# Seven-product feed-forward on one core: in the first unit the third and fourth product change places, and VectorE makes the fourth's input difference first

## The chip, the core and the metric

The kernel runs on one NeuronCore of one Trainium2 chip. The metric is the device time of one execution in microseconds (us), from runs on the chip; less is better. The core's engines run apart and meet at semaphores: TensorE (PE in the profile, with its weight loads as PEld), VectorE (DVE), ScalarE (ACT), GpSimd (POOL) and SyncE (SP), which issues most of the DMAs.

## The reference

A first network of two layers works on 256 tokens of width 1024: a feed-forward, a mixer (two attentions and a gated delta rule), a second feed-forward. A second network of two layers follows, with a context stream beside it, and its own feed-forward. All is float32. What bears on this change are the feed-forwards:

```
def swiglu(h, w_gu, w_down):
    gate, up = jnp.split(h @ w_gu, 2, axis=-1)
    return (jax.nn.silu(gate) * up) @ w_down

def squared_relu_mlp(h, w1, w2):
    return jnp.square(jax.nn.relu(h @ w1)) @ w2

for l in range(DEPTH):                                   # first network
    x = x + 0.5 * swiglu(rmsnorm(x, ffn1_norm[l]), ffn1_w_gu[l], ffn1_w_down[l])
    x = x + hybrid_mixer(rmsnorm(x, mix_norm[l]), ...)
    x = x + 0.5 * swiglu(rmsnorm(x, ffn2_norm[l]), ffn2_w_gu[l], ffn2_w_down[l])
ctx = ctx + cgt2 * squared_relu_mlp(modulate(rms_norm(ctx, g2), csh2, csc2), w1, w2)
x = x + gt2 * squared_relu_mlp(modulate(rms_norm(x, g2), sh2, sc2), w1, w2)
```

The squared-ReLU form runs once for the context and twice for x, so there are seven feed-forwards in all.

## The kernel before

Each feed-forward is cut into units (17 in the first network, 16 in the second), one slot of weights each. A unit is a matrix product done in the seven-product way of Strassen and Winograd: the weights are four quarters `a11, a12, a21, a22`, the input is `low` (its first four tiles) and `high`, each split into tokens 0 to 127 (`tok0`) and 128 to 255 (`tok1`). Three differences of the input serve all the up units: `t1 = low[tok1] - low[tok0]`, `t2 = high[tok1] - t1`, `t4 = high[tok0] - t2`; a fourth, `high[tok1] - low[tok1]`, is written over `low[tok1]`. VectorE makes them, four instructions of 128x512 in each feed-forward, and counts each on `x_diffs`. It also makes four sums of weight quarters in each unit, counted on `sums_made`: two in `early_sums` (the second, L2077, puts `a11 - a21` over `a21`), one in `sum_two` (L2091), one in `sum_four` (L2097).

TensorE runs the products of unit k in the order p1 and p2 (`raw`), p6, p7, p5 (`middle`), then p1 and p2 of unit k+1, then p4 and p3 (`end`). So the third product is p6, the fourth p7. p6 takes t2 and the sum of L2091; p7 takes `low[tok1]`'s difference and the sum of L2077, and writes another PSUM bank (`v_bank`, in `spots`) than p1, p6, p5 and p3, which add up in one (in `units`). Between p6 and p5 ScalarE copies that bank out (`u2_kept`): p5 may not start before. After p5 it is copied again (`u4_kept`).

```
e_.wait_ge(*p6_done.at(c, base + k + 1))
activate(u2s[k % 2], mu_bank(c, which, k), ACT.Copy).then_inc(u2_kept.handle, 1)
```

All engines run this order as written; there is no scheduler. In the first network TensorE also sums up squares for the norm (`square_sums`, L813) in the first unit: before p6 in the very first one, right behind p6 in the other three. ScalarE waits for that sum, makes Ln and Exp of it (`res_root`), and only then comes to the copy `u2_kept`. In the very first unit it waits, ahead of the copy, for the condition vector from DRAM (`cond_here`). The four first-network units hold eight matrix instructions of 128x256 in a product in the trace; the three of the second network sixteen of 128x128.

Of the kernel before, what the change touches and what calls it, by code (L numbers as in the profile page):

```python
# [21 lines left out]
ALU = mybir.AluOpType  # L22
# [4 lines left out]
P = 128  # L27
T = 256
# [262 lines left out]
def build(nc, stream, x_in, ctx_in, cond, positions, vec1, vec2, bada, consts, tables, out):  # L291
    with ExitStack() as ctx:
# [6 lines left out]
        def signal(name, first=0, **counts):  # L299
            return Signal(sem(name), counts, first)  # L300
# [109 lines left out]
        w_bank, v_bank = spot[:, 4, 0:T], spot[:, 5, 0:T]  # L410
# [11 lines left out]
        p1_done, p2_done, p4_done, p5_done, p6_done, p7_done = (signal(f"product{i}_done", **MUS) for i in (1, 2, 4, 5, 6, 7))  # L422
        p3_done = signal("product3_done", SLOTS, **MUS)
        sums_made = signal("weight_sums_made", **{k: 4 * n for k, n in MUS.items()})
        c1_kept, u2_kept, u4_kept = (signal(f"{n}_kept", **MUS) for n in ("c1", "u2", "u4"))
        c11_made, c21_made = (signal(f"{n}_made", 1, **MUS) for n in ("c11", "c21"))
        c22_made = signal("c22_made", **MUS)
        x_taken = signal("chain_bank_taken", 2, **MUS)
        x_diffs = signal("input_differences_made", one=8, ctx=4, two=4)
# [107 lines left out]
        def input_sum(c, which):  # L537

            if which:
                return c, 1  # L540
            return (Place("one", c.turn - 1), 2) if c.turn else (Place("load"), 0)
# [8 lines left out]
        def mu_half(c, k):  # L550

            return 4 if (c.sec != "one" or k < FFN_UP) else DOWN_HALF[(k - FFN_UP) % 3]
# [4 lines left out]
        def mu_quarters(c, which, k):  # L557


            w, n = slot[(MU_GROUP[c.sec][which] + k) % SLOTS], mu_half(c, k)  # L560
            if k < mu_up(c):
                w = w[:, :].rearrange("p (e k h m c) -> p h m e k c", e=2, k=n, h=2, m=2)
                return w[:, 0, :, 0], w[:, 0, :, 1], w[:, 1, :, 0], w[:, 1, :, 1]
            w = w[:, 0:8 * n * P].rearrange("p (h m k e c) -> p h m e k c", h=2, m=2, k=n, e=2)
            return w[:, 0, :, 0], w[:, 0, :, 1], w[:, 1, :, 0], w[:, 1, :, 1]

        def by_tokens(c, k):

            return c.sec == "one" and k < FFN_UP

        def mu_sum(c, k):

            n = mu_half(c, k)
            return w_sum["one" if c.sec == "one" else "two"][k % 2][:, 0:2 * n * P].rearrange("p (m k c) -> p m k c", m=2, k=n)

        def mu_moving(c, which, k):

            if k < mu_up(c):
                return lambda kt: (act[:, kt, :], act[:, 4 + kt, :], kt)
            chunk = (k - mu_up(c)) % (3 if c.sec == "one" else 4)  # L580
            return lambda kt: (hT[:, 8 * chunk + 2 * kt, :], hT[:, 8 * chunk + 2 * kt + 1, :], 4 * chunk + kt)

        def mu_bank(c, which, k):

            return lin[:, (k + 1 + which) % 2 if c.sec == "one" else k % 2, 0:T]

        def mu_diffs(c, k):

            return x_diff if k < mu_up(c) else h_diff["one" if c.sec == "one" else "two"]
# [167 lines left out]
        def _(pe):  # L757
# [82 lines left out]
            def multiply(c, which):  # L840

                count, up = MUS[c.sec] // len(MU_GROUP[c.sec]), mu_up(c)
                base = count * which
# [7 lines left out]
                def quarter(dst, weights, n, moving, first, rows_=False):  # L851

                    if rows_:
                        for kt in range(n):
                            mm = pe.matmul(dst.rearrange("p (m c) -> p m c", m=2), moving(kt), weights[:, :, kt, :], start=(first and kt == 0),  # L855
                                           stop=(kt == n - 1), skip_group_check=True)
                        return mm
                    for m in range(2):
                        for kt in range(n):
                            mm = pe.matmul(dst[:, m * P:m * P + P], weights[:, m, kt, :], moving(kt),  # L860
                                           start=(first and m == 0 and kt == 0), stop=(kt == n - 1), skip_group_check=True)
                    return mm
# [7 lines left out]
                def raw(k):  # L870
# [22 lines left out]
                    if opening:  # L893
                        square_sums(*input_sum(c, which))

                def middle(k):
                    (a11, _, a21, _), n = mu_quarters(c, which, k), mu_half(c, k)
                    moving, (t1, t2, _) = mu_moving(c, which, k), mu_diffs(c, k)
                    if k == 0:
                        pe.wait_ge(*x_diffs.at(c, 4 * which + 2))  # L900
                    pe.wait_ge(*c1_kept.at(c, base + k + 1))
                    pe.wait_ge(*sums_made.at(c, 4 * (base + k) + 3))
                    quarter(mu_bank(c, which, k), a11, n, lambda kt: t2[:, moving(kt)[2], :], False, by_tokens(c, k)
                            ).then_inc(p6_done.handle, 1)
                    if k == 0 and c.sec == "one" and (c.turn or which):
                        square_sums(*input_sum(c, which))
                    if k == 0:
                        pe.wait_ge(*x_diffs.at(c, 4 * which + 4))
                    pe.wait_ge(*c21_made.at(c, base + k))
                    quarter(v_bank, a21, n, lambda kt: moving(kt)[0][:, P:T], True, by_tokens(c, k)).then_inc(p7_done.handle, 1)  # L910
                    pe.wait_ge(*u2_kept.at(c, base + k + 1))
                    quarter(mu_bank(c, which, k), mu_sum(c, k), n, lambda kt: t1[:, moving(kt)[2], :], False,
                            by_tokens(c, k)).then_inc(p5_done.handle, 1)

                def end(k):
                    (_, a12, _, a22), n = mu_quarters(c, which, k), mu_half(c, k)
                    moving, (_, _, t4) = mu_moving(c, which, k), mu_diffs(c, k)
                    pe.wait_ge(*c22_made.at(c, base + k + 1))
                    quarter(v_bank, a22, n, lambda kt: t4[:, moving(kt)[2], :], False, by_tokens(c, k)
                            ).then_inc(p4_done.handle, 1)  # L920
                    pe.wait_ge(*u4_kept.at(c, base + k + 1))
                    pe.wait_ge(*sums_made.at(c, 4 * (base + k) + 4))
                    quarter(mu_bank(c, which, k), a12, n, lambda kt: moving(kt)[1][:, P:T], False, by_tokens(c, k)
                            ).then_inc(p3_done.handle, 1)
# [559 lines left out]
            def two(c, order):  # L1484
                for step, i in order:
                    if step == "sum":
                        square_sums(c, i)
                    elif step == "lin":
                        plain_two(c, *i)
                    elif step in ("scores", "turn", "values", "out", "early"):  # L1490
                        {"scores": scores_two, "turn": turn_two, "values": values_two, "out": out_two,
                         "early": early}[step](c, i)
                    elif step == "csum":
                        pe.wait_ge(*c21_made.at(Place("ctx"), TWO_MU))
                        square_sums(Place("ctx"), 1)
                    elif step == "klin":
                        key_product(c, i)
                    elif step not in ("norm", "squares", "soft", "gsum", "gmul", "knormed", "ksquare"):
                        rest_two(c, step)
                multiply(c, 0)  # L1500
# [4 lines left out]
            for l in range(DEPTH):  # L1505
                c = Place("one", l)
                multiply(c, 0)
                if l == 0:
                    pe.wait_ge(consts_made, 1)
                mixer(c)  # L1510
                multiply(c, 1)
# [460 lines left out]
        def _(ve):  # L1972
# [106 lines left out]
            def multiply(c, which):  # L2079
                count, up = MUS[c.sec] // len(MU_GROUP[c.sec]), mu_up(c)  # L2080
                base = count * which
# [5 lines left out]
                def sum_two(k):  # L2087
                    a11 = mu_quarters(c, which, k)[0]
                    ve.drain()
                    ve.wait_ge(*p1_done.at(c, base + k + 1))  # L2090
                    ve.tensor_tensor(a11, mu_sum(c, k), a11, ALU.subtract).then_inc(sums_made.handle, 1)  # L2091
# [17 lines left out]
                low, high, tok0, tok1 = act[:, 0:4, :], act[:, 4:8, :], slice(0, P), slice(P, T)  # L2109

                def second_difference():
                    ve.tensor_tensor(t2, high[:, :, tok1], t1, ALU.subtract).then_inc(x_diffs.handle, 1)

                ve.drain()
# [21 lines left out]
                    ve.wait_ge(*normed.at(c, 2 * KD))  # L2136
                    second_difference()
                sum_two(0)
                ve.tensor_tensor(low[:, :, tok1], high[:, :, tok1], low[:, :, tok1], ALU.subtract).then_inc(x_diffs.handle, 1)
                if first and which == 0:  # L2140
                    before, i = input_sum(c, which)
                    if added_up(before, i):
# [561 lines left out]
            for l in range(DEPTH):  # L2704
                c = Place("one", l)
# [171 lines left out]
```

## Time and profile before

| | us |
|---|---|
| median of 3 runs | 2614.05 (2613.34 to 2615.8) |
| the profiled execution, its own time | 2619.14 |
| its span, first to last instruction | 2617.3 |
| PE busy | 2580.3 (99%) |
| PEld busy | 2273.3 (87%) |
| DVE busy | 1390.8 (53%) |
| ACT busy | 746.5 (29%) |
| POOL busy | 19.3 (1%) |

The mean granted TensorE clock is 0.997 of full speed. A row of the timeline gives its start, its length, engine, line, operation, what it writes and reads with shapes, how many instructions are merged, and in brackets how long the engine was idle before and what released it. The seven first units are called A to G here, by the start of p6:

| first unit | part of the network | p6 starts, us |
|---|---|---|
| A | layer 1, first feed-forward | 17.99 |
| B | layer 1, second feed-forward | 622.18 |
| C | layer 2, first feed-forward | 840.80 |
| D | layer 2, second feed-forward | 1443.51 |
| E | context | 1765.70 |
| F | second network, layer 1 | 2092.15 |
| G | second network, layer 2 | 2415.96 |

### The profile page before, as it was taken

Reading aid. Unit: us, or ns where it says so; the run is one execution under the profiler, and the core shown is the slowest. Engines: PE = TensorE matmul, PEld = TensorE weight load, DVE = VectorE, ACT = ScalarE, POOL = GpSimd, SP = SyncE. Lnnn points to the kernel's source line nnn. Section 1 sums busy time; section 2 is a strip of 40 time slices with the busy share of each in tenths; the row PEclk is TensorE's granted clock in tenths of the full one; section 3 lists DMA queues with packets and bytes.
Section 4 is the critical chain, followed back from the end, with each engine's and each line's share of the span. In section 5 each row is a group of like instructions: output and inputs, shape, how many; then the busy total and the mean of one; then the engine's idle time right before and its main releaser. Section 6 shows DMA issues by size and latency. Waiting matters only on the chain.

```text
span 2617.3 us, 46846 instructions
## 1 busy us (share of the span) xinstructions
PE 2580.3 (99%) x19506; PEld 2273.3 (87%) x19506; DVE 1390.8 (53%) x2373; ACT 746.5 (29%) x1825; POOL 19.3 (1%) x33
## 2 busy tenths in 40 slices
PE   9999999999999999999999999999999999999999
PEld 7899778888899889787888889869997799967999
DVE  6674253315666666244422666256663566635665
ACT  4531132112541551123210453231123411133110
POOL 0000000000000000000000000000000000000000
PEclk9999999999999999999999999999999999999999
DMA  7664321145555565431135565424443144431443
GB/s 264 226 226 180 118 89 73 69 158 203 215 218 218 200 231 208 150 121 49 67 121 188 228 225 210 167 97 142 180 170 136 68 150 177 162 129 65 161 162 113
DMA packets 54483, 414.71 MB, mean 158 GB/s; under 512 B 4128, under 2 KB 8480, under 8 KB 34432
## 3 DMA queue, kind: packets, MB, share of 16 engines
q1 hardware_dynamic: 50224, 357.96, 37.2%
q10 hardware_dynamic: 3456, 50.33, 5.2%
q8 instruction: 155, 2.54, 0.4%
q0 software_dynamic: 592, 3.41, 0.4%
q14 instruction: 56, 0.46, 0.0%
HBM read 410.64 MB, written 1.05 MB: 157 GB/s over the span
## 4 chain that ended last, share of the span: by engine, by line
PE 95%; DVE 2%; ACT 1%; DVEq 1%; issue 0%; DMA 0%; ACTq 0%; SPq 0%
PE units L860 19%; PE spots L860 14%; PE units L781 14%; PE units L855 12%; PE spots L855 8%; PE units L986 7%; PE spots L1176 2%; PE units L1287 2%; PE spots L836 2%; PE units L1334 2%; PE units L1452 1%; PE units L964 1%; PE units L957 1%; PE spots L1383 1%; PE spots L1364 1%; PE spots L1373 1%
## 5 line engine op out<-in xcount | busy, mean ns | idle before, releaser
L781 PE MATMUL units<-normed,weights 128*128 128x256 f32 x1040 | 230.6, 382 | 2.2 <-ACT normed L1523 2.2
L1523 ACT ACTIVATE mla_q_rope<-units 128x256 f32<-128x256 f32 (+1 forms) x248 | 95.4, 387 | 461.5 <-PE units L860 368.9
L781 PEld LDWEIGHTS units<-normed,weights 128*128 128x128 f32 x1040 | 197.8, 191 | 32.5 <-issue 5.9
L1523 ACT ACTIVATE hidden<-delta_qkv 32x128 f32<-32x128 f32 x704 | 215.5, 306 | 7.7
L986 PE MATMUL units<-normed,weights 128*128 128x256 f32 x832 | 191.9, 384 | 0.0
L860 PE MATMUL units<-hidden,weights 128*128 128x128 f32 x1472 | 180.9, 276 | 0.0
L860 PE MATMUL spots<-hidden,weights 128*128 128x128 f32 x1472 | 180.1, 275 | 0.0
L986 PEld LDWEIGHTS units<-normed,weights 128*128 128x128 f32 x832 | 154.5, 190 | 28.8 <-issue 8.0
L860 PEld LDWEIGHTS units<-hidden,weights 128*128 128x128 f32 x1472 | 172.1, 192 | 1.6 <-issue 1.6
L860 PEld LDWEIGHTS spots<-hidden,weights 128*128 128x128 f32 x1472 | 172.1, 192 | 0.0
L855 PE MATMUL units<-weights,normed 128*128 128x256 f32 x704 | 167.6, 381 | 1.6 <-DMA weights<-stream 1.6
L855 PE MATMUL spots<-weights,normed 128*128 128x256 f32 x704 | 167.3, 381 | 0.7 <-DMA weights<-stream 0.5
L855 PEld LDWEIGHTS spots<-weights,normed 128*128 128x128 f32 x704 | 134.5, 191 | 20.0 <-DMA weights<-stream 0.9
L855 PEld LDWEIGHTS units<-weights,normed 128*128 128x128 f32 x704 | 132.6, 190 | 21.6 <-issue 4.1
L2097 DVE TENSOR_TENSOR weights<-weights 128x1024 f32<-128x1024 f32 (+1 forms) x116 | 140.0, 1207 | 10.7
L2198 DVE TENSOR_TENSOR delta_new_values<-spots,mla_q_rope 128x256 f32<-128x256 f32 x116 | 49.1, 423 | 176.0 <-PE spots L860 154.2
L2077 DVE TENSOR_TENSOR weights<-weights 128x1024 f32<-128x1024 f32 (+1 forms) x116 | 139.1, 1199 | 0.0
L1523 ACT ACTIVATE delta_state<-units 128x256 f32<-128x256 f32 x116 | 44.6, 384 | 279.2 <-PE units L860 220.2
L781 PE MATMUL units<-hidden,weights 128*128 128x256 f32 x528 | 119.4, 382 | 0.6 <-DVE residual L2689 0.4
L781 PEld LDWEIGHTS units<-hidden,weights 128*128 128x128 f32 x528 | 98.7, 190 | 16.4 <-issue 3.0
L860 PE MATMUL units<-normed,weights 128*128 128x128 f32 x768 | 95.9, 279 | 5.0 <-ACT normed L1523 4.4
L2091 DVE TENSOR_TENSOR weights<-latents,weights 128x1024 f32<-128x1024 f32 (+1 forms) x56 | 67.6, 1207 | 60.0 <-PE units L860 35.0
(389 smaller groups left out, 4160.7 us busy)
## 6 DMA issues: line engine op xcount, KB each, us to landing
weights<-stream SPq DMA_DIRECT2D x138, 2048.0 KB, 7.7
values_mla_qk_mla_values<-stream ACTq DMA_DIRECT2D x24, 2048.0 KB, 8.2
weights<-stream SPq DMA_DIRECT2D x46, 1024.0 KB, 5.2
weights<-stream SPq DMA_DIRECT2D x16, 768.0 KB, 7.1
weights<-stream SPq DMA_DIRECT2D x4, 512.0 KB, 8.7
constants<-consts SPq DMA_DIRECT2D x1, 1094.5 KB, 14.0
residual<-x_in SPq DMA_DIRECT2D x2, 512.0 KB, 5.8
weights<-stream SPq DMA_DIRECT2D x4, 256.0 KB, 5.1
```

The source lines that it names most:

```text
L781: mm = pe.matmul(dst, w[:, kt * width + col:kt * width + col + P], rhs[:, kt, :], start=(kt == 0), stop=(kt == k - 1))
L836: mm = pe.matmul(banks[32 * q:32 * q + 32, 0, 0:P], cond_s[:, kt, :], w, start=(kt == 0), stop=(kt == KD - 1))
L855: mm = pe.matmul(dst.rearrange("p (m c) -> p m c", m=2), moving(kt), weights[:, :, kt, :], start=(first and kt == 0), stop=(kt == n - 1), ...
L860: mm = pe.matmul(dst[:, m * P:m * P + P], weights[:, m, kt, :], moving(kt), start=(first and m == 0 and kt == 0), stop=(kt == n - 1), skip ...
L986: mm = pe.matmul(dst[:, m * T:m * T + T], w[:, col:col + P], act[:, kt, :], start=(kt == 0), stop=(kt == KD - 1), skip_group_check=True)
L1176: mm = pe.matmul(banks[rows_, t, col:col + CHUNK], lhs[rows_, t, e, p, :], stacked[rows_, :] if rhs is None else rhs[rows_, t, e, p, :], s ...
L1287: mm = pe.matmul(dst[:, m * T:m * T + T], w[:, col:col + P], merged[:, kt, :], start=(kt == 0), stop=(kt == KD - 1))
L1334: mm = pe.matmul(dst, act[:, kt, part * P:part * P + P], w[:, kt * 512:kt * 512 + 512], start=(kt == 0), stop=(kt == KD - 1))
L1523: return nc.scalar.activation(dst, src, func, **kw)
L2077: ve.tensor_tensor(a21, a11, a21, ALU.subtract).then_inc(sums_made.handle, 1)
L2091: ve.tensor_tensor(a11, mu_sum(c, k), a11, ALU.subtract).then_inc(sums_made.handle, 1)
L2097: ve.tensor_tensor(a12, a12, a11, ALU.subtract).then_inc(sums_made.handle, 1)
```

## The change

In the first unit of every feed-forward TensorE runs p7 ahead of p6. VectorE makes the difference for p7 right ahead of t2, where it stood behind `sum_two`. The counts that p7 and p6 wait for on `x_diffs` are fitted to that, and the wait for t4 moves from p7 to p4. The other units are as they were.

```
+                def seventh(k, a21, n, moving):
+                    if k == 0:
+                        pe.wait_ge(*x_diffs.at(c, 4 * which + 2))
+                        pe.wait_ge(*sums_made.at(c, 4 * (base + k) + 2))
+                    pe.wait_ge(*c21_made.at(c, base + k))
+                    quarter(v_bank, a21, n, lambda kt: moving(kt)[0][:, P:T], True, by_tokens(c, k)).then_inc(p7_done.handle, 1)
+
                 def middle(k):
                     (a11, _, a21, _), n = mu_quarters(c, which, k), mu_half(c, k)
                     moving, (t1, t2, _) = mu_moving(c, which, k), mu_diffs(c, k)
                     if k == 0:
-                        pe.wait_ge(*x_diffs.at(c, 4 * which + 2))
+                        seventh(k, a21, n, moving)
+                        pe.wait_ge(*x_diffs.at(c, 4 * which + 3))
...
                     if k == 0 and c.sec == "one" and (c.turn or which):
                         square_sums(*input_sum(c, which))
-                    if k == 0:
-                        pe.wait_ge(*x_diffs.at(c, 4 * which + 4))
-                    pe.wait_ge(*c21_made.at(c, base + k))
-                    quarter(v_bank, a21, n, lambda kt: moving(kt)[0][:, P:T], True, by_tokens(c, k)).then_inc(p7_done.handle, 1)
+                    if k:
+                        seventh(k, a21, n, moving)
...
                     pe.wait_ge(*c22_made.at(c, base + k + 1))
+                    if k == 0:
+                        pe.wait_ge(*x_diffs.at(c, 4 * which + 4))
...
                 def second_difference():
+                    ve.tensor_tensor(low[:, :, tok1], high[:, :, tok1], low[:, :, tok1], ALU.subtract).then_inc(x_diffs.handle, 1)
                     ve.tensor_tensor(t2, high[:, :, tok1], t1, ALU.subtract).then_inc(x_diffs.handle, 1)
...
                 sum_two(0)
-                ve.tensor_tensor(low[:, :, tok1], high[:, :, tok1], low[:, :, tok1], ALU.subtract).then_inc(x_diffs.handle, 1)
```

On TensorE, in unit B (layer 1, second feed-forward), the order before, where `spots<-weights1,normed` is p2 at its first place and p7 at its second, `units<-weights1,squares` is p6 and `units<-rows,squares` is p5:

```order
L1287 MATMUL units<-delta_qkv,weights0 128x256 x32
L855 MATMUL units<-weights1,normed 128x256 x4
L855 MATMUL spots<-weights1,normed 128x256 x4
L855 MATMUL units<-weights1,squares 128x256 x4
L813 MATMUL spots<-square_sums,ones 128x256
L855 MATMUL spots<-weights1,normed 128x256 x4
L855 MATMUL units<-rows,squares 128x256 x4
L855 MATMUL units<-weights2,normed 128x256 x4
```

and now:

```order
L1295 MATMUL units<-delta_qkv,weights0 128x256 x32
L855 MATMUL units<-weights1,normed 128x256 x4
L855 MATMUL spots<-weights1,normed 128x256 x8
L855 MATMUL units<-weights1,squares 128x256 x4
L813 MATMUL spots<-square_sums,ones 128x256
L855 MATMUL units<-rows,squares 128x256 x4
L855 MATMUL units<-weights2,normed 128x256 x4
```

p7 now stands right behind p2 (together the x8), and p5 comes directly behind p6 and the sum of squares; C and D read the same, and in A the sum stands ahead of both.

On VectorE, at the same place, the order before, where L2112 makes t2, L2091 is `sum_two`, L2139 makes the difference over `low[tok1]` and L2146 makes t4:

```order
L2003 TENSOR_TENSOR square_sums<-square_sums,squares 128x256 x2
L2112 TENSOR_TENSOR squares<-normed,squares 128x512
L2091 TENSOR_TENSOR weights<-rows,weights 128x2x4x128
L2139 TENSOR_TENSOR normed<-normed 128x4x128
L2146 TENSOR_TENSOR squares<-normed,squares 128x512
L2097 TENSOR_TENSOR weights<-weights 128x2x4x128
```

and now, each line number 8 higher or, from L2112 to L2121, 9 higher:

```order
L2011 TENSOR_TENSOR square_sums<-square_sums,squares 128x256 x2
L2120 TENSOR_TENSOR normed<-normed 128x4x128
L2121 TENSOR_TENSOR squares<-normed,squares 128x512
L2099 TENSOR_TENSOR weights<-rows,weights 128x2x4x128
L2154 TENSOR_TENSOR squares<-normed,squares 128x512
L2105 TENSOR_TENSOR weights<-weights 128x2x4x128
```

The difference of L2139 moved ahead of t2 and of `sum_two` (now L2099); t4 and `sum_four` have the same work ahead of them as before.

## Rows read from the trace of the kernel before

**Rows 1.** The page's chain that ended last, shares of the span by engine.
```profile
PE 95%; DVE 2%; ACT 1%; DVEq 1%; issue 0%; DMA 0%; ACTq 0%; SPq 0%
```

**Rows 2.** Timeline of B: start us, us, engine, line, operation, count [idle before].
```profile
619.46 1.26 DVE L2112 TENSOR_TENSOR squares<-normed,squares 128x512 f32<-128x512 f32 x1
...
621.96 0.68 DVE L2139 TENSOR_TENSOR normed<-normed 128x512 f32<-128x512 f32 x1
...
622.18 3.65 PE L855 MATMUL units<-weights,squares 128*128 128x256 f32 x8 [2.33 <-DVE weights L2091]
622.56 0.68 DVE L2146 TENSOR_TENSOR squares<-normed,squares 128x512 f32<-128x512 f32 x1
...
626.30 0.38 ACT L1523 ACTIVATE rstd<-spots 128x256 f32<-128x256 f32 x1 [6.46 <-PE spots L813]
...
627.26 0.38 ACT L1523 ACTIVATE mla_q_rope<-units 128x256 f32<-128x256 f32 x1
...
627.83 1.89 PE L855 MATMUL units<-rows,squares 128*128 128x256 f32 x8
```

**Rows 3.** Timeline of C, the same columns.
```profile
837.86 1.13 DVE L2112 TENSOR_TENSOR squares<-normed,squares 128x512 f32<-128x512 f32 x1
838.58 0.99 POOL L722 TENSOR_TENSOR square_sums<-square_sums,squares 128x256 f32<-128x256 f32 x1
...
840.80 1.97 PE L855 MATMUL units<-weights,squares 128*128 128x256 f32 x8 [1.51 <-DVE weights L2091]
...
843.23 0.38 ACT L1523 ACTIVATE rstd<-spots 128x256 f32<-128x256 f32 x1 [4.48 <-PE spots L813]
...
844.02 0.37 ACT L1523 ACTIVATE mla_q_rope<-units 128x256 f32<-128x256 f32 x1
...
844.76 1.89 PE L855 MATMUL units<-rows,squares 128*128 128x256 f32 x8
```

**Rows 4.** Timeline of A.
```profile
14.16 1.22 DVE L2076 TENSOR_TENSOR rows<-weights 128x1024 f32<-128x1024 f32 x1 [0.84 <-DMA weights<-stream]
...
15.31 1.22 DVE L2077 TENSOR_TENSOR weights<-weights 128x1024 f32<-128x1024 f32 x1
...
17.99 3.65 PE L855 MATMUL units<-weights,squares 128*128 128x256 f32 x8 [2.91 <-DVE weights L2091]
...
22.37 0.42 ACT L1523 ACTIVATE context_keys<-context_keys 128x256 f32<-128x256 f32 x1 [5.07 <-DMA context_keys<-cond]
...
22.70 0.37 ACT L1523 ACTIVATE mla_q_rope<-units 128x256 f32<-128x256 f32 x1
...
23.20 1.91 PE L855 MATMUL units<-rows,squares 128*128 128x256 f32 x8
```

**Rows 5.** Timeline of E: p6.
```profile
1765.70 2.02 PE L860 MATMUL units<-squares,weights 128*128 128x128 f32 x16 [0.75 <-DVE weights L2091]
```

**Rows 6.** Timeline of F: p2, p6, the copy of ScalarE, p5.
```profile
2090.11 1.95 PE L860 MATMUL spots<-normed,weights 128*128 128x128 f32 x16
...
2092.15 2.02 PE L860 MATMUL units<-squares,weights 128*128 128x128 f32 x16
...
2094.21 0.38 ACT L1523 ACTIVATE mla_q_rope<-units 128x256 f32<-128x256 f32 x1 [3.52 <-PE units L860]
...
2095.79 1.95 PE L860 MATMUL units<-squares,probabilities 128*128 128x128 f32 x16
```

**Rows 7.** Timeline: p1 of E and of G, each behind an idle time.
```profile
1760.29 2.49 PE L860 MATMUL units<-normed,weights 128*128 128x128 f32 x16 [2.21 <-ACT normed L1523]
...
2410.55 3.66 PE L860 MATMUL units<-normed,weights 128*128 128x128 f32 x16 [2.21 <-ACT normed L1523]
```

**Rows 8.** Stretches right behind idle times: A:B, us, PE busy, granted clock, DMA share, GB/s.
```profile
622.20:625.60 3.40, 3.40 (x8) 0.50 0.29 119
1760.30:1763.70 3.40, 3.28 (x23) 1.00 0.52 217
2410.80:2414.20 3.40, 3.40 (x17) 0.50 0.43 183
```

## The prediction, written before the changed kernel ran

> **What bounds the kernel now.** I read the chain of waits first: 95% of the span lies on TensorE [rows 1], so only what delays or frees a matrix product counts, and an instruction moved on VectorE costs nothing unless a product waits behind it. Then I read the timeline around the seven first units. The reader is to see one pattern in it. In B TensorE had p2 done at 619.85 and stood idle for 2.33 us, until `sum_two` had made the weights of p6 [rows 2]. C has the same wait with 1.51 us, A with 2.91, E with 0.75 [rows 3 to 5]. F has hardly any: p6 starts 2.04 us behind p2, where two products behind it together take 3.64, so 1.82 each; 0.22 are lost [rows 6]. D repeats B row for row, 2.33 us idle too, and G repeats F with a still smaller gap. The third thing to read is the second half of the same rows: p5 never waits for its input in B to G, because p7 stands between p6 and p5 and covers ScalarE's copy. The fourth is the clock. Right behind B's gap the granted clock was 0.50 for 3.4 us, which is 1.2 GHz of 2.4; behind C's gap p6 took 1.97 us instead of B's 3.65, so it ran at 2.4 GHz [rows 2, 3, 8].
>
> All starts below are moved on the profiled execution's time line. Its own time was 2619.14 for a span of 2617.3; the median of the runs shown is 2614.05. I form the difference on the trace and add it to the median.
>
> **What the change moves on VectorE.** One instruction, `low[tok1]`'s difference, 0.68 us long, goes ahead of t2 and `sum_two`. Two such in a row start 0.60 apart (L2139 at 621.96, L2146 at 622.56) [rows 2]. So `sum_two` and with it p6 become ready 0.60 later wherever VectorE was busy up to there (B to G). t4, `sum_four` and what follows keep their time, since the same work lies ahead of them. No DMA and no queue of SyncE or GpSimd is passed. In A the move is free: VectorE idled 0.84 there for a weight piece (L2076) [rows 4]. The wait for t4, moved from p7 to p4, is met several products before and costs nothing.
>
> **What it moves on TensorE.** p7 fills the gap ahead of p6, a product's length that is no longer needed later. Against that p5 loses its cover. From now on p5 starts when ScalarE has copied p6's bank. In the second network that is p6's start to the copy's start, 2.06, the copy 0.38, and about 0.13 to the first product (copy end 23.07, p5 at 23.20 in A), so 2.57 instead of 3.64 [rows 4, 6]. In the first network the sum of squares, Ln and Exp stand ahead of the copy on ScalarE's queue. In C: p6 840.80, Ln 843.23, copy 844.02 to 844.39, plus 0.13, gives 3.72 from p6 to p5, where it is 3.96 now [rows 3]. In B Ln to copy is 0.96 and not 0.79 [rows 2], which gives 2.43 + 0.96 + 0.38 + 0.13 = 3.90.
>
> **B and D.** The first of the three VectorE instructions takes 1.26 us in B, stretched beside an add of GpSimd as in C [rows 2, 3]. Now the moved difference is in its place: 619.46 + 1.26 = 620.72, and p7 starts 0.15 later (the trace's usual distance to VectorE's end) at 620.87, behind a gap of 1.02. It ends about 622.8. p6 is ready at 622.18 + 0.60 = 622.78. No gap as long as 2.33 is left, and C's 1.51 brought no fall of the clock, so p6 runs at 2.4 GHz. p5 starts at 622.78 + 3.90 = 626.68, before at 627.83 [rows 2]: a gain of 1.15. All of it comes from the clock: with the clock up p5 would have started at 622.18 + 3.96 = 626.14 before, and the change would then lose 0.54. D the same: in sum 2.3 gained.
>
> **C.** The gap of 1.51 holds p7 nearly whole; p6 starts at 841.40, p5 at 841.40 + 3.72 = 845.12, before 844.76: 0.4 lost [rows 3].
>
> **E, F, G.** In E TensorE is free at 1764.95; p7 takes 1.82, p5 follows 2.57 behind p6: 1769.34. Before it was 1765.70 + 3.64 = 1769.34: nothing [rows 5, 6]. In F p7 could start at 2090.11 + 1.82 = 2091.93, p6 at 2093.75, p5 at 2096.32, before 2095.79: 0.5 lost [rows 6]. G as F: 0.5 lost.
>
> **A.** p5 starts at 23.20 because ScalarE is held until 22.37 by the condition vector's DMA, and only then copies p6's bank (22.70) [rows 4]. Neither moves, so p5 starts at 23.20 again. But p7 can begin at 15.31 + 1.22 + 0.15 = 16.68, p6 follows, and both are done near 20.3 if the clock holds. So TensorE's gap of 2.91 doesn't go, it moves from ahead of p6 to ahead of p5. Before, the two products at 1.2 GHz were hidden by the DMA; now a fall of the clock hits p5 and what follows, all of which lies on the path. The price of a fall is B's p6 to p5, 5.65, less C's 3.96: 1.7 [rows 2, 3]. A gap of 2.91 at this place had a fall (p6 took 3.65) [rows 4], so I count it: 1.7 lost. The bounds are 0 and 1.7.
>
> Sum: -2.3 + 0.4 + 0 + 0.5 + 0.5 + 1.7 = 0.8 us slower, so 2614.05 + 0.8, about 2614.9. The later waits of TensorE are set by VectorE and ScalarE, which follow TensorE's own products, so a shift passes through to the end.
>
> **Two rules weighed.** The rows show that a gap of 2.21 us ahead of E's p1 left the granted clock at 1.00 and one of the same 2.21 ahead of G's p1 brought 0.50 [rows 7, 8]. By the Trainium skill, TensorE: Matmul & The Clock Gate, section "What's actually happening", the observation of activity runs on by itself and does not start anew with the kernel, so where a gap lands decides. By that rule the falls of B and D need not be in the timed runs at all, and neither need A's; the rows of E and G agree with it. It is the second rival below.
> In C the first of VectorE's instructions took 1.13 us and the next GpSimd add ran from 838.58 to 839.57 [rows 3]. The Trainium skill's page SBUF — State Buffer, section "Who interferes with whom", says that a VectorE instruction with two inputs in SBUF and a GpSimd one that reads there block each other for a whole instruction. By that rule t2 in C would start only at 839.57, and C's loss would be 0.7 and not 0.4.
>
> **Rivals.** First, nothing falls in A: the gap ahead of p5 is cut in two by where it lands, or p7 itself runs slowly behind the 1.60 us that stay idle ahead of it and the DMA hides that again. For it: E's gap passed. Against it: both longest gaps of the trace, A's and B's, had a fall. Time: 2614.9 - 1.7 = 2613.2.
> Second, this one clearly on the slower side: the lost cover decides alone. It does so where B's and D's gaps had no fall in the timed runs; then there is no clock to win back, and each loses 0.54 instead of gaining 1.15. Its place is p5's wait for the copy in six first units, its price 0.54 + 0.54 + 0.4 + 0.5 + 0.5 = 2.5, with A's fall 4.2. It decides from the point where p6's start moves by less than the clock had cost. Time: 2616.5 to 2618.2, the middle 2617.4. For it: the runs shown are 3 to 6 us quicker than the profiled one.
> Third, faster: p7 in the gap ends the falls in B and D, A has none, and ScalarE's chain is quicker than I read it, so that nothing is lost in C, F and G: -1.15 - 1.15, time 2611.8. For it: ScalarE is busy for 29% of the span only. Against it: the copy's place behind p6 is in the code and in every row.
> Fourth, new falls: behind p5's new wait, some 1.4 us in B, C and D (p6's start plus about 2.3 of work against 3.7 to 3.9), the clock falls. Each costs 1.7: 2614.9 + 5.1 = 2620.0. Against it: C's gap of 1.51 had none.
> Fifth, the change does not do what it says, p7 waiting for something else (the copy out of its bank, the weights' sum): the order shows that it waits only for work done long before, so this has next to no chance.
>
> **How the numbers follow.** The forecast has 0.40, the first rival 0.15, the second 0.28, the third 0.07, the fourth 0.08, the fifth 0.02. About 0.2%, 5.2 us, is what a measurement of this kernel can tell from no change. The range, 2612.0 to 2618.6, takes in the forecast and the first two rivals and leaves out the third and the fourth, 0.15 of the chance. Faster by over 5.2 us no case reaches: 0.02 for what I don't see. Slower by over 5.2 takes nearly all of the fourth rival (2620.0): 0.06. Within it, 0.92.
>
> **What would show it.** In the changed profile p7 starts within 0.2 us of the moved difference's end in B and D, p6 0.6 later than before, and p5 is released by ScalarE's copy in B to G, with idle time of TensorE ahead of it. In B and D the granted clock stays at 1.00; in A it falls behind 22 us. In A p5 starts at 23.2. If p5 in B starts before 626 or TensorE is not idle ahead of it in C, my reading of ScalarE's queue is wrong; a total beyond 2620 or below 2611 would mean something outside these seven places.

## The result and the profile after

The changed kernel takes 2618.95 us (median of 20 runs, 2618.12 to 2621.17), the kernel before 2615.48 (20 runs, 2613.31 to 2617.73): ratio 1.0016, 95% interval 1.001 to 1.0022, so 3.5 us slower by the medians and some 4 by the ratio, where 0.8 was forecast. 2618.95 lies 0.35 us above the stated range and 4.05 above the forecast of 2614.9; 1.43 of that is the base, since the forecast was added to 2614.05, the median of three runs, and twenty runs gave 2615.48. The profiled execution of the changed kernel took 2618.94 us, its span is 2617.1, and TensorE still carries 95% of the chain [rows 1].

In B the change did what the rows of before promised. Timeline of the changed kernel, same columns as [rows 2]:

```profile
618.61 1.26 DVE L2120 TENSOR_TENSOR normed<-normed 128x512 f32<-128x512 f32 x1
...
619.92 1.99 PE L855 MATMUL spots<-weights,normed 128*128 128x256 f32 x8 [0.93 <-DVE normed L2120]
...
621.93 1.97 PE L855 MATMUL units<-weights,squares 128*128 128x256 f32 x8
...
624.36 0.38 ACT L1531 ACTIVATE rstd<-spots 128x256 f32<-128x256 f32 x1 [5.38 <-PE spots L813]
...
625.32 0.38 ACT L1531 ACTIVATE mla_q_rope<-units 128x256 f32<-128x256 f32 x1
...
625.76 1.99 PE L855 MATMUL units<-rows,squares 128*128 128x256 f32 x8 [1.44 <-ACT mla_q_rope L1531]
```

p7 starts 0.05 us behind the moved difference, p6 runs at full clock (1.97 us), and p5 has a wait of its own, 1.44 us, for ScalarE's copy. p6 to p5 takes 3.83 (3.90 forecast).

In C, against [rows 3], p6 waits 0.55 and p5 1.24:

```profile
839.61 1.97 PE L855 MATMUL units<-weights,squares 128*128 128x256 f32 x8 [0.55 <-DVE weights L2099]
...
843.25 1.99 PE L855 MATMUL units<-rows,squares 128*128 128x256 f32 x8 [1.24 <-ACT mla_q_rope L1531]
```

VectorE there, ahead of p6, with GpSimd's add (POOL) beside the two differences:

```profile
835.88 1.13 DVE L2120 TENSOR_TENSOR normed<-normed 128x512 f32<-128x512 f32 x1
836.61 0.99 POOL L722 TENSOR_TENSOR square_sums<-square_sums,squares 128x256 f32<-128x256 f32 x1
836.94 1.21 DVE L2121 TENSOR_TENSOR squares<-normed,squares 128x512 f32<-128x512 f32 x1
```

t2 took 1.21 us instead of 0.69: it ended 0.55 behind the add. This agrees with the rule of the Trainium skill, SBUF — State Buffer, section "Who interferes with whom", that the prediction weighed. C's measured loss, 0.56, lies between the prediction's two sums, 0.4 and 0.7. The second counted the add's cost as new, but the same add had cost VectorE time before the change too, in `sum_two`, which took 1.57 us there instead of 1.22:

```profile
839.08 1.57 DVE L2091 TENSOR_TENSOR weights<-rows,weights 128x1024 f32<-128x1024 f32 x1
```

With t2 from 839.57, `sum_two` 0.60 later at its plain 1.22 and 0.15 to p6, the second sum comes to 841.54 for p6 and 845.26 for p5, a loss of 0.5 and not 0.7. From the first difference to p6 that is 3.68 us; it measured 3.73.

In A the gap has moved ahead of p5, against [rows 4], but p5 ran at full clock in this record:

```profile
15.77 1.97 PE L855 MATMUL spots<-weights,normed 128*128 128x256 f32 x8 [1.57 <-issue]
...
22.26 1.99 PE L855 MATMUL units<-rows,squares 128*128 128x256 f32 x8 [2.80 <-ACT mla_q_rope L1531]
```

G costs more than the 0.5 forecast. Before, p1 to p6 were 2410.55 to 2415.96, 5.41 us [rows 7]; now it is 7.52, with p7 in between (p2 and p7 are one row). To compare like with like, take p1 to p5, which holds p7 in both orders: 9.06 before and 9.95 now. p5 before:

```profile
2419.61 1.95 PE L860 MATMUL units<-squares,probabilities 128*128 128x128 f32 x16
```

and G now (the view ends inside p5):

```profile
2409.40 3.47 PE L860 MATMUL units<-normed,weights 128*128 128x128 f32 x16 [2.21 <-ACT normed L1531]
2412.66 4.43 PE L860 MATMUL spots<-normed,weights 128*128 128x128 f32 x32
2416.92 1.95 PE L860 MATMUL units<-squares,weights 128*128 128x128 f32 x16
2419.35 0.82 PE L860 MATMUL units<-squares,probabilities 128*128 128x128 f32 x5 [0.47 <-ACT mla_q_rope L1531]
```

The clock, in the columns of [rows 8], is down behind three gaps, of E's p1, of a place near 2294 us that the change doesn't touch (the first projection of the second network's last layer, L781), and of G's p1:

```profile
1758.80:1762.10 3.30, 3.30 (x17) 0.50 0.24 99
2294.70:2298.00 3.30, 3.30 (x10) 0.50 0.28 119
2410.70:2414.00 3.30, 3.30 (x17) 0.50 0.10 40
```

### The profile page after: what moved, and what is told of

It is laid out like the page before. It is cut to its first block, busy times and chain, and to the rows that moved or that the text cites. A ratio compares the mean times of both kernels' runs of the same rounds, so it can differ in the third digit from the quotient of the medians.

```text
span 2617.1 us, 46853 instructions
## 1 busy us (share of the span) xinstructions
PE 2578.7 (99%) x19506; PEld 2270.9 (87%) x19506; DVE 1390.9 (53%) x2373; ACT 746.7 (29%) x1825; POOL 19.2 (1%) x33
## 3 DMA queue, kind: packets, MB, share of 16 engines
HBM read 410.64 MB, written 1.05 MB: 157 GB/s over the span
## 4 chain that ended last, share of the span: by engine, by line
PE 95%; DVE 2%; ACT 1%; DVEq 1%; DMA 1%; issue 0%; SPq 0%; ACTq 0%
PE units L860 19%; PE spots L860 14%; PE units L781 14%; PE units L855 11%; PE spots L855 8%; PE units L994 7%; PE spots L1184 2%; PE units L1295 2%; PE spots L836 2%; PE units L1342 2%; PE units L1460 1%; PE units L972 1%; PE units L965 1%; PE spots L1391 1%; PE spots L1372 1%; DMA context_keys<-cond 1%
## 5 line engine op out<-in xcount | busy, mean ns | idle before, releaser
L781 PE MATMUL units<-normed,weights 128*128 128x256 f32 x1040 | 230.7, 382 | 2.2 <-ACT normed L1531 2.2
L781 PEld LDWEIGHTS units<-normed,weights 128*128 128x128 f32 x1040 | 197.8, 191 | 32.5 <-issue 5.9
L781 PE MATMUL units<-hidden,weights 128*128 128x256 f32 x528 | 119.4, 382 | 0.6 <-DVE residual L2697 0.4
L781 PEld LDWEIGHTS units<-hidden,weights 128*128 128x128 f32 x528 | 98.7, 190 | 16.4 <-issue 3.0
L2099 DVE TENSOR_TENSOR weights<-latents,weights 128x1024 f32<-128x1024 f32 (+1 forms) x56 | 67.6, 1207 | 59.6 <-PE units L860 35.0
```

What stands on the lines that cost most here:

```text
L781: mm = pe.matmul(dst, w[:, kt * width + col:kt * width + col + P], rhs[:, kt, :], start=(kt == 0), stop=(kt == k - 1))
```

## The experiments

"Before" beside a result is the kernel before on the same chip in the same session. Where an experiment's own records are read, the places keep the names A to G.

**before_again.** No edit.

> The kernel before once more, for a second record of where its clock falls. If the first profile was typical of the timed runs: falls in A, B, D, near 2294 and in G again. If it was not (its time, 2619.14, lies above all timed runs): fewer, with B or D or both at full clock, where p6 to p5 then takes 3.96 us instead of 5.65.

It took 2615.42 us, the median of the runs of before beside it, so by its time this record is the typical one. Granted clock behind D's p6 gap, E's p1, the place near 2294 (2292.77 in this record) and G's p1:

```profile
1443.00:1446.40 3.40, 3.25 (x15) 1.00 0.97 410
1758.90:1762.20 3.30, 3.30 (x17) 0.50 0.32 134
2292.80:2296.20 3.40, 3.40 (x16) 1.00 0.55 236
2407.50:2410.80 3.30, 3.30 (x17) 0.50 0.32 134
```

D and the place near 2294 are at full clock here, where the first record had a fall in both; B and A have one again. In D p6 to p5 is 3.96, so the forecast's "with the clock up" case holds there:

```profile
1443.15 1.97 PE L855 MATMUL units<-weights,squares 128*128 128x256 f32 x8 [2.33 <-DVE weights L2091]
...
1447.11 1.89 PE L855 MATMUL units<-rows,squares 128*128 128x256 f32 x8
```

And E had a fall, yet p1 to p6 took 5.53 us, against 5.41 without one in the first record:

```profile
1758.22 3.64 PE L860 MATMUL units<-normed,weights 128*128 128x128 f32 x16 [2.21 <-ACT normed L1523]
1761.65 2.26 PE L860 MATMUL spots<-normed,weights 128*128 128x128 f32 x16
1763.75 1.95 PE L860 MATMUL units<-squares,weights 128*128 128x128 f32 x16
```

TensorE's wait for `sum_two` (0.75 in E, [rows 5]) had swallowed the slow p1.

**change_again.** No edit of the changed kernel.

> The changed kernel once more, on the chip and beside the runs of before that the other kernels share. Theory 1 (lost cover): p5 waits for ScalarE's copy in B, C, D, F and G, some 2.5 us in all, and the falls of the clock in B and D that the profile of before shows are absent from most timed runs, so nothing is won back: 2.5 us slower plus what falls elsewhere add, 2.5 to 4. Theory 2 (clock): the waits themselves cost little; the changed kernel has one or two falls of the clock more than before (A's gap ahead of p5; E and G), 1.7 us each, so its mean granted clock is lower than that of before by 0.0007 or more in the runs, and its times stand in two groups some 1.8 us apart. My forecast's theory (falls in B and D won back) expects 0 to 1 us.

2619.2 us (11 runs) against 2615.28 (31): ratio 1.0016, 1.0007 to 1.0025. Five runs lie at 2620.0 to 2620.9 with a mean granted clock of 0.997, six at 2618.1 to 2619.2 with 0.998. At 0.998 the kernel before averages 2614.9 (14 runs), at 0.997 2616.0 (13 runs). So at equal clock the change still costs 4.0 and 4.6 us: more falls cannot be the main difference. What a fall costs and the lost cover remain. The record is of the upper group, 1.74 above the first one, and in A its p5 ran at half clock:

```profile
22.48 3.44 PE L855 MATMUL units<-rows,squares 128*128 128x256 f32 x8 [3.19 <-ACT mla_q_rope L1531]
```
```profile
22.90:26.20 3.30, 3.30 (x10) 0.50 0.70 293
```

**vector_only.** VectorE's part alone (shortened):

```
 def middle(k):
-    pe.wait_ge(*x_diffs.at(c, 4 * which + 2))       # ahead of p6
+    pe.wait_ge(*x_diffs.at(c, 4 * which + 3))
 def second_difference():
+    ve.tensor_tensor(low[:, :, tok1], high..., low..., ALU.subtract)...   # no longer behind sum_two
```

> Only VectorE's part of the change: low's difference ahead of t2; TensorE keeps p6 before p7. Theory 1: p6 waits for sum_two, so it starts 0.6 us later in B, C, D and E and some 0.4 later in F and G, 3.2 us slower in all, A unchanged; the whole change must then have won about 0.7 back on TensorE. Theory 2: the longer gap ahead of p6 (2.9 in B and D, 2.1 in C) brings falls of the clock too, 4.5 to 8 us slower.

2621.94 us (9 runs) against 2615.28: ratio 1.0025, 1.0015 to 1.0035. The size is that of theory 2, the clock: C's gap grew from 1.51 to 2.30 and now has a fall (p6 3.34 us long).

```profile
843.13 3.34 PE L855 MATMUL units<-weights,squares 128*128 128x256 f32 x8 [2.30 <-DVE weights L2091]
```
```profile
840.20:843.50 3.30, 1.00 (x5) 1.00 1.04 442
843.60:846.90 3.30, 3.30 (x9) 0.50 0.58 248
```

So TensorE's part of the change wins back some 2.7 us of the 6.7 that VectorE's costs.

**only_second.** The whole change where `c.sec != "one"`, so in E, F and G:

```
+def seventh_first(c, which):
+    return c.sec != "one"
```

with both orders kept in the code under this condition (the same in only_bd, only_a, without_a).

> The whole change in E, F and G alone (second network and context), A to D as before. Theory 1: 0 in E and 0.5 each in F and G, 1.0 us slower. Theory 2: a fall of the clock ahead of p1 in E and G was partly hidden by the wait ahead of p6, which p7 now fills, so up to 0.9 in E, 0.4 in F and 1.0 in G, 2.3 us slower.

2617.53 (11 runs) against 2615.28: ratio 1.0008, 0.9999 to 1.0016. The median lies at theory 2's 2.3, but the interval, 0.3 us faster to 4.2 slower, holds theory 1's 1.0 as well and doesn't tell them apart.

**only_bd.** `return c.sec == "one" and which == 1`.

> The whole change in B and D alone. Theory 1: p5 0.54 us later in each where the clock holds in before, so 1.1 us slower in most timed runs. My forecast's theory (the gap of 2.33 costs a fall of the clock in each before, and the change ends it): 2.3 us faster. With a fall in only some of the runs of before, between: the two balance where a third of the gaps had one.

2616.45 (11 runs) against 2615.28: ratio 1.0003, 0.9994 to 1.0012. The interval, 1.6 us faster to 3.1 slower, excludes the gain of 2.3; 1.1 slower fits.

**only_a.** `return c.sec == "one" and which == 0 and c.turn == 0`.

> The whole change in A alone. If the gap of 2.9 us ahead of p5 matters by the clock only: its times stand in two groups, at those of before and 1.7 us above, the mean 0.5 to 1 us slower. If nothing in A matters (the DMA of the condition vector hides it all): as before.

2618.24 (11 runs) against 2615.42 (27): ratio 1.0009, 1.0 to 1.0018. More than expected, and not in two clean groups. The record shows p5 at half clock, 3.47 us long:

```profile
22.66 3.47 PE L858 MATMUL units<-rows,squares 128*128 128x256 f32 x8 [2.82 <-ACT mla_q_rope L1536]
```

**without_a.** The change everywhere but in A.

> The whole change in B to G, with A as before. The changed kernel's times stand in two groups 1.8 us apart, and its two profiles differ by a fall of the clock ahead of p5 in A (22.87 us) that costs 1.7. If that fall makes the upper group: the upper group goes, most runs at 2618 to 2619, the mean 0.7 us below the changed kernel's. If A plays no part in the whole change: the two groups stay.

2618.19 (11 runs, 2616.99 to 2619.36) against 2615.23 (15): ratio 1.0011, 1.0002 to 1.002. The group above 2620 is gone, so A makes it; of the whole 3.5 to 3.9 us A has some 0.5 to 1.

**before_warm** and **change_warm.** Seven products of ones ahead of p1 in E and G, in the kernel before and in the changed one:

```
+if c.sec in ("ctx", "two"):
+    for _ in range(7):
+        pe.matmul(w_bank[:, 0:P], ones[:, :], ones[:, :], start=True, stop=True, skip_group_check=True)
 raw(0)
```

> The kernel before with seven products of ones (result unused, into the bank that p2 fills next) in the 2.21 us ahead of p1 in E and G, so that the clock doesn't fall there. If a fall ahead of p1 in E and G is hidden by the wait ahead of p6 (p1 to p6 took 5.41 us in E without a fall and 5.41 in G with one), this changes nothing: within 0.5 us of before, p1 to p6 again 5.41. If a fall costs its 1.7 wherever it comes, up to 3.4 us faster.

> The changed kernel with the same seven products in E and G. If p7 has taken the wait that hid the fall, this wins 1.0 us in E and 1.0 in G: p1 to p6 near 6.5 us in both (was 7.45 and 7.52), 2 us faster than the changed kernel, 2 slower than before. If the loss in E and G is the wait for ScalarE's copy alone, it stays at the changed kernel's time.

before_warm: 2614.97 (11 runs) against 2615.42 (27), ratio 1.0, 0.9991 to 1.0009. change_warm: 2616.87 (11 runs), ratio 1.0003, 0.9994 to 1.0012, 2.3 below change_again. No clock fell in E or G of either record. In before_warm p1 in G takes 2.49 us and not 3.66, and in its place TensorE waits 0.75 for `sum_two` ahead of p6: p1 to p6 is 5.42, p1 to p5 9.06, both as with the fall (the view ends inside p5):

```profile
2406.38 2.49 PE L860 MATMUL units<-normed,weights 128*128 128x128 f32 x16 [0.65 <-ACT normed L1526]
...
2411.80 2.02 PE L860 MATMUL units<-squares,weights 128*128 128x128 f32 x16 [0.75 <-DVE weights L2094]
...
2415.44 0.72 PE L860 MATMUL units<-squares,probabilities 128*128 128x128 f32 x5
```

In change_warm p1 to p6 is 6.29 in G, not 7.52, and p1 to p5 is 8.71, not 9.95:

```profile
2408.59 2.49 PE L860 MATMUL units<-normed,weights 128*128 128x128 f32 x16 [0.66 <-ACT normed L1534]
2410.91 4.12 PE L860 MATMUL spots<-normed,weights 128*128 128x128 f32 x32
2414.88 1.95 PE L860 MATMUL units<-squares,weights 128*128 128x128 f32 x16
2417.30 2.05 PE L860 MATMUL units<-squares,probabilities 128*128 128x128 f32 x16 [0.47 <-ACT mla_q_rope L1534]
```

The same edit is worth 0.45 us in the one kernel, which is nothing within its interval of 2.4 either way, and over 2 in the other. With the records this shows that the wait filled by p7 had been hiding the falls. It shows too that with the clock up the change is no loss in E and G up to p5: 8.71 against 9.06.

**sums_first** and **change_sums_first.** The sum of squares of B, C and D ahead of p6, in the kernel before and in the changed one (behind p7):

```
+if k == 0 and c.sec == "one" and (c.turn or which):
+    square_sums(*input_sum(c, which))
 quarter(mu_bank(c, which, k), a11, n, ...).then_inc(p6_done.handle, 1)
-if k == 0 and c.sec == "one" and (c.turn or which):
-    square_sums(*input_sum(c, which))
```

> The kernel before, with the sum of squares of B, C and D ahead of p6 instead of behind it, in the gap where TensorE waits for sum_two. If p5 is set by TensorE's own order there, it starts 0.43 us earlier in each (the sum's length), p6 to p5 3.5 and not 3.96: 1.3 us faster, and a little more where the shorter gap ahead of p6 spares a fall. If a fall comes all the same in the runs, nothing measurable.

> The changed kernel with the same move: p7, sum of squares, p6, p5. Ln and Exp then lie beside p6, and p5 waits for the plain copy only, 2.5 us behind p6 as in E to G, not 3.7 to 3.9. If ScalarE's queue is what p5 waits for in B, C and D: p5 1.2 us earlier in B and D and 0.9 in C, 2.5 to 3.3 us faster than the changed kernel, still about 1 slower than before by A, E, F and G. If p5's wait is something else there, as the changed kernel.

sums_first: 2614.02 (11 runs) against 2615.12 (27), ratio 0.9996, 0.9987 to 1.0004: of the expected size, not told from nothing. change_sums_first: 2616.83 (11 runs), ratio 1.0008, 0.9999 to 1.0017. Ln no longer stands between p6 and the copy, and p5 follows p6 by 2.36 instead of 3.83:

```profile
624.43 1.89 PE L855 MATMUL units<-weights,squares 128*128 128x256 f32 x8
626.79 0.48 PE L855 MATMUL units<-rows,squares 128*128 128x256 f32 x1 [0.47 <-ACT mla_q_rope L1531]
```

**best_bd.** `seventh_first` for B and D, and the sum ahead of p6 in B, C and D.

> p7 first in B and D only, and the sum of squares ahead of p6 in B, C and D; A, C, E, F and G keep p6 first. By the rows p5 in B starts at about 625.5 on the first profile's line, where sums_first would give 625.75 and before 626.14 with the clock up: 1.7 us faster than before in all, and no gap over 1.1 us left in B and D for the clock to fall in. If falls in B and D cost before's runs on average half of 1.7 each, it gains that too: up to 3.4 us faster.

2612.47 us (11 runs, 2611.08 to 2613.93) against 2615.12 (27): ratio 0.999, 0.9981 to 0.9999. It beats both kernels, the one before by 2.6 us; the interval just leaves out no change. In B no gap is over 0.93, and p5 is 2.36 behind p6:

```profile
619.52 1.99 PE L858 MATMUL spots<-weights,normed 128*128 128x256 f32 x8 [0.93 <-DVE normed L2126]
621.36 0.59 PE L816 MATMUL spots<-square_sums,ones 128*128 128x256 f32 x2
621.79 1.89 PE L858 MATMUL units<-weights,squares 128*128 128x256 f32 x8
...
624.15 2.00 PE L858 MATMUL units<-rows,squares 128*128 128x256 f32 x8 [0.47 <-ACT mla_q_rope L1536]
```

## Why the prediction was wrong

The two typical records are before_again (2615.42) and the first of the changed kernel (2618.94). The table takes the start of the same ScalarE instruction, a copy of TensorE's bank, in both, behind each place: after minus before, and what the place added.

| behind | shift, us | added | forecast |
|---|---|---|---|
| start and A | -0.5 | -0.5, in change_again with its fall 1.9 more | 1.7 |
| B | -1.6 | -1.1 | -1.15 |
| C | -1.05 | 0.56 | 0.4 |
| D | -0.45 | 0.6 | -1.15 |
| E | 0.4 | 0.9 | 0 |
| F | 0.9 | 0.4 | 0.5 |
| place near 2294 | 2.5 | 1.7 | not seen |
| G | 3.5 | 1.0 | 0.5 |

The end of the span is 3.53 later, the two times differ by 3.52. The -0.5 of the first row is no gain of the change: p5 in A starts 0.36 apart in the two records of the kernel before as well (23.20 and 22.84).

**What held.** The path is TensorE's. The moved difference delays p6 by 0.6, p7 fills the gap, p5 waits for ScalarE's copy, and the chain Ln, Exp, copy sets that wait in B, C and D (in change_sums_first p5 comes 1.2 us sooner behind p7). B with a fall before, C and F came within 0.2 of their terms. D without a fall lost 0.6, where the text had 0.54 for that case. That p5's new waits of 1.2 to 1.4 bring a fall (the fourth rival) did not show: none of the five records that have them in B and D, and none of the four in C, has one there.

**"D the same: in sum 2.3 gained"** failed. It took one record's falls for those of all runs, though that record (2619.14) lay above every timed run. The unchanged gap of 2.33 had a fall in B in all five records that kept it, and in D in two of them. In the timed runs the interval of only_bd excludes the 2.3.

**"G as F" and "In E ... nothing"** failed: 1.0 and 0.9. I priced E and G as if only ScalarE's copy changed. But their p1 runs behind a gap of 2.21, nearly always slowly, and the wait ahead of p6 paid for that: p1 to p6 took 5.41 in G with a fall and 5.41 in E without [rows 5, 7]. The equality stood in the rows, and I read past it. With p7 in the wait's place it is 7.52 with a fall and 6.29 without. before_warm and change_warm show this directly: p1 to p5 in G is 9.06 with a fall and without in the kernel before, 9.95 and 8.71 in the changed one.

**A** was mis-sized: the fall was counted as certain at 1.7. It came in three of the five records with p7 first in A (change_again, only_a, change_sums_first), and in 8 of the 20 runs the time is of the upper group. By without_a A is worth some 0.5 to 1 us of the whole.

**The place near 2294** was not in the forecast at all, see below.

The second rival's difference, 2.5 to 4.2 us slower, holds the measured 3.5 (its times, 2616.5 to 2618.2, stand on the low base of 2614.05 and do not hold 2618.95). Part of that is luck: the lost cover of p5 is its C, D and F, but the rest of the 3.5 is falls in E and G that had been free and one more near 2294, which it did not have.

What stays open: how often B and D have a fall in the timed runs (B's five of five and D's two of five would make only_bd a gain of some 1.2; it measured 1.2 slower, and its interval holds both), why only_a costs 2.8 where without_a leaves 0.5 to 1 for A, and what brings the fall near 2294, which is 1.7 of the 3.5 between the two records.

## What to carry to other kernels

An idle stretch on the bounding engine may be paying for something else, here for a product slowed down just before it. Before filling it, compare the time across it in places with and without the slow product: if it is the same, the stretch is not free. And work taken out from between a product and its reader's wait must be counted as cover: look at what the other engine does first in its queue. A record that lies above all timed runs is not the one to take clock falls from.

## What the runs showed of the hardware

The granted clock fell behind G's gap of 2.21 us in all twelve records that left it open, behind E's in ten of them, and never behind the gaps of 1.43 to 1.51 in B, C and D. Two far places went together. In six records E's p1 starts 534.5 to 534.8 us ahead of the place near 2294, with both gaps of 2.21 open, and exactly one of the two had a fall in each. In the other six with both open the distance is 535.6 to 535.9, and both had one. Five of these have the change in E to G, which moves the two 1.3 us apart (0.9 in E, 0.4 in F). The sixth is vector_only, where TensorE's order is as before and the distance 535.7, so the shift goes with the second fall also without p7 ahead of p6. A fall near 2294 costs 1.7. So a small shift at one place may decide on a fall 500 us later, which the kernel's own rows there don't show. No run made the shift alone, so that it is the cause is not shown.
